# Moving eight modulation rows behind the expert loop, and ten weight slots into the second mixer

## The chip, the cores and the metric

The program runs on one core of a Trainium2 chip. The metric is the device time of one execution, in microseconds. Before the change the median of three runs is 1236.26 us (1230.97 to 1237.36). The profiled execution took 1236.48 us; its span, from the first to the last instruction, is 1234.6 us.

## The reference, cut to what matters

```python
c_act = jax.nn.silu(c)
for l in range(DEPTH):                       # DEPTH = 2, 256 tokens, width 1024, float32
    mod = (c_act @ w_mod[l] + b_mod[l])[:, None, :]
    sh1, sc1, g1, sh2, sc2, g2 = jnp.split(mod, 6, axis=-1)
    y = hybrid_mixer(x * (1.0 + sc1) + sh1, ...)
    x = layer_norm(DN_ALPHA * x + (1.0 + g1) * y, ln_g[l, 0], ln_b[l, 0])
    h = x * (1.0 + sc2) + sh2
    y = swiglu(h, ...) if l == 0 else moe_swiglu(h, ...)   # moe: top 2 of 8 experts, each 1024 x 2816 (gate, up), 2816 x 1024 (down)
    x = layer_norm(DN_ALPHA * x + (1.0 + g2) * y, ln_g[l, 1], ln_b[l, 1])
```

Each of the twelve modulation vectors is a product of one vector with a 1024 x 1024 block of w_mod. The last one, g2 of the second layer, multiplies the output of the experts and is used nowhere else.

## The kernel before, in words

The kernel goes through mixer 0, a dense feed-forward of 11 steps, mixer 1, a short routing part and the experts. All engine programs are written out by hand in order, one block for each engine, and semaphores order them against each other. SyncE (SP) issues nearly all loads.

**The modulation rows.** A modulation vector (number m) is built from 8 "rows", each a [128, 1024] block of w_mod (512 KB). VectorE multiplies each row by a column of c_act and adds it to mod_acc[m % 2] (condition_rows, L1549 to L1566; s["row_rd"] counts the rows done). TensorE then sums over the 128 partitions with a matrix of ones (gate_sum, L1012 to L1016), and VectorE adds bias and 1 (gate_apply, L1508 to L1516). Rows 64 to 71 belong to gate 10, g1 of the second layer, which the layer norm behind mixer 1 needs. Rows 72 to 79 belong to gate 11, g2 of the second layer. SP loads rows 72 to 79 in load_mod_rows (L396 to L422) behind the last weight unit of mixer 1.

**The end of mixer 1.** The output projection has four weight units (u = 12 to 15, here called i = 0 to 3). Each is split by ScalarE and VectorE into a high and a low part (conv_unit, low_unit) and used by TensorE in 3-pass products (project_out, L1104). TensorE does i = 0 and 1 for both token tiles, then gate_sum(10), then for token tile t = 0 and 1 the units i = 2 and 3, each 24 products; gate_sum(11) stands between i = 2 and 3 of t = 1. s["proj"] counts units finished for t = 1. VectorE's order (L1768 to L1781) is: rows 69 to 71, low part of i = 2, rows 72 to 75, gate_apply(10), low part of i = 3, rows 76 to 79, layer_norm(2). layer_norm (L1576) takes the four half tiles (t, h) in turn; half h = 1 of a tile needs i = 2 and 3 (for t = 0: s["wo"]; for t = 1: s["proj"]), and behind the second tile's statistics it runs gate_apply(11).

**The experts.** All weights of 8 experts stream once through a ring of 14 slots, raw_w, of 1 MB each. One expert takes 35 slots in the order: gate and up tiles of a chunk (8 slots), down tiles of the chunk before (4, 4, 3). The chunks of 2816 columns are 1024, 1024 and 768 wide. Expert loads are issued by SP: a slot is loaded again as soon as TensorE has finished with it (slot_free, L484, on s["m_used"]). The first 8 slots are the first chunk of expert 0, loaded behind s["yT_L"] >= 8; the other 6 wait for the whole mixer (s["proj"] >= 2 * NU). TensorE runs the first chunk, then a loop over pairs of experts (three rounds), then the last pair written out behind the loop (experts 6 and 7). Gate and up products are at L1399, down products at L1413. Between experts, ScalarE and VectorE add the rows of an expert (expert_rows), ScalarE stores them to DRAM (slots) and loads the tokens of a later expert (x_rows). TensorE's first down tile of an expert waits for expert_rows (s["m_y1"]). GpSimd (POOL) issues four indirect stores of tokens at the start of the experts (L647, s["sent"]) and then waits for the last pair, where it gathers the results back.

The slots overlap buffers of mixer 1: slots 0 to 4 lie on the mixer's attention buffers, slots 5 and 6 partly on buffers of rows 69 to 71, slots 8 and 9 on the raw buffers of weight units i = 0 and 1, slots 10 to 13 on those of the later units.

Of the kernel before, what the change touches and what calls it, by code (L numbers as in the profile page):

```python
# [24 lines left out]
P = 128  # L25
D = 1024
KT = D // P
T = 256
TT = T // P
# [27 lines left out]
FREE = 8  # L57
LAST1, LAST2 = NE // 2 - 1, PASSES * NE // 2 - 1
# [29 lines left out]
ROWS_DENSE, ROWS_MIX1 = 24, 64  # L88
# [12 lines left out]
           + YC + HF + [YC0, X0 + 6, X0 + 4, X0 + 5] + HF + [X0 + i for i in range(4)] + HF)  # L101
# [10 lines left out]
def hybrid_decoder(nc, x, c, w_in, w_a2, b_a, gla_norm_g, w_out, w_mod, b_mod, ln_g, ln_b,  # L112
# [3 lines left out]
    with ctx:  # L116
# [173 lines left out]
        last_S = place("last_S", [P, GROUPS, T], at=hTH_at)  # L290
        y_last = place("y_last", [P, GROUPS, 512], at=hfull_at)
# [38 lines left out]
        def rows_done(n):  # L330

            return n - sum(i < n for i in PE_ROWS)
# [51 lines left out]
        def _(sp):  # L384
# [8 lines left out]
            def load_mod_rows(*rows):  # L393

                for n in rows:
# [11 lines left out]
                    if n in (12, 72):  # L407
                        sp.wait_ge(s["pv_ps"], 2 * mix + 2)
# [4 lines left out]
                    if n == 74:  # L413
                        sp.wait_ge(s["yT_L"], 8)
# [9 lines left out]
            def unit_load(l, u):  # L424
# [10 lines left out]
                for src, at in unit_parts(l, u):  # L435
# [4 lines left out]
                               {5: (64, 65), 8: (66, 67), 9: (68, 69, 70, 71), 15: (72, 73)})  # L440
# [39 lines left out]
            load_mod_rows(*range(74, len(MOD_ROWS)))  # L480

            mg, mu, md = moe_w_gate[0], moe_w_up[0], moe_w_down[0]
            sp.wait_ge(s["yT_L"], 8)
# [6 lines left out]
            def load_gate_up(e, pr, n, c):  # L490

                f = slice(CHUNK_AT[c], CHUNK_AT[c] + CHUNK_W[c])
                for k in range(KT):
# [29 lines left out]
            load_gate_up(0, 0, -FIRST, 0)  # L523
            sp.wait_ge(s["proj"], 2 * NU)
# [19 lines left out]
        def _(pool):  # L544
# [104 lines left out]
            pool.wait_ge(s["x_ln"], 6)  # L649
            pool.wait_ge(s["m_end"], 1)  # L650
# [324 lines left out]
        def _(pe):  # L975
# [36 lines left out]
            def gate_sum(m, banks):  # L1012
# [135 lines left out]
            def mixer(l):  # L1148
# [90 lines left out]
                for t in range(TT):  # L1239
                    for i in (2, 3):  # L1240
# [10 lines left out]
                        elif l and t and i == 2:  # L1251
                            pe.wait_ge(s["row_rd"], rows_done(len(MOD_ROWS)))
                            gate_sum(11, (0, 3))
# [96 lines left out]
            pe.wait_ge(s["modT"], 11)  # L1350
# [97 lines left out]
            pe_expert(n_last, 0, True, False)  # L1448
            pe_expert(n_last, 1, True, True)
# [15 lines left out]
        def _(dve):  # L1465
# [84 lines left out]
            def condition_rows(rows):  # L1550

                for n in rows:
                    m, l, a, k = MOD_ROWS[n]
                    row, acc = mod_row[int(n >= ROWS_MIX1)][ROW_BUF[n]], mod_acc[m % 2][:]
                    dve.wait_ge(row_ld[ROW_BUF[n]], row_landed(n))
# [20 lines left out]
            def layer_norm(ph, terms):  # L1576
# [19 lines left out]
                if ph == 2:  # L1596
                    gate_apply(11, (0, 3), gate3_row)
# [122 lines left out]
            def mixer(l):  # L1720
# [52 lines left out]
                condition_rows(range(72, 76) if l else range(12, 14))  # L1773
                if l:
                    gate_apply(10, (1, 2), g_row)
                low_unit(l, NIN + 3)
                condition_rows(range(76, 80) if l else range(14, 16))
                if l == 0:
# [280 lines left out]
```

## Time and profile before

| | |
|---|---|
| median of 3 runs | 1236.26 us (1230.97 to 1237.36) |
| the profiled execution | 1236.48 us, span 1234.6 us |
| TensorE, share busy | 93% |
| VectorE, share busy | 44% |
| ScalarE, share busy | 23% |
| GpSimd, share busy | 5% |
| DMA traffic | 423.12 MB, mean 343 GB/s |
| chain that ended last | TensorE 69%, VectorE 5%, issue 2%, DMA 2%, ScalarE 1% |
| granted TensorE clock, mean | 0.984 of full speed |

The second mixer ends at about 504 us, the routing part at 521 us, and the experts fill the rest. "PE" is TensorE, "DVE" VectorE, "ACT" ScalarE, "POOL" GpSimd, "SPq" the queue of SyncE. A DMA share is the mean busy share of the core's 16 DMA engines; it reads slightly over 1 when all are busy.

### The profile page before, as it was taken

Reading aid. Unit: us, or ns where it says so; the run is one execution under the profiler, and the core shown is the slowest. Engines: PE = TensorE matmul, PEld = TensorE weight load, DVE = VectorE, ACT = ScalarE, POOL = GpSimd, SP = SyncE. Lnnn points to the kernel's source line nnn. Section 1 sums busy time; section 2 is a strip of 40 time slices with the busy share of each in tenths; the row PEclk is TensorE's granted clock in tenths of the full one; section 3 lists DMA queues with packets and bytes.
Section 4 is the critical chain, followed back from the end, with each engine's and each line's share of the span. In section 5 each row is a group of like instructions: output and inputs, shape, how many; then the busy total and the mean of one; then the engine's idle time right before and its main releaser. Section 6 shows DMA issues by size and latency. Waiting matters only on the chain.

```text
span 1234.6 us, 25919 instructions
## 1 busy us (share of the span) xinstructions
PE 1149.0 (93%) x11052; PEld 656.3 (53%) x11052; DVE 540.1 (44%) x884; ACT 283.6 (23%) x486; POOL 67.3 (5%) x118
## 2 busy tenths in 40 slices
PE   1889899999999898699999999999999999999995
PEld 1789777778878798423333324334334344343342
DVE  6799867777768999740121111021111201201226
ACT  0556343333426563310010010010100100100100
POOL 3100010000112000010000000000000000000011
PEclk9999999999999999899999999999999999999998
DMA  9974778999956747999999999999999999999991
GB/s 344 311 254 137 270 259 315 350 371 397 335 180 195 264 137 248 409 385 369 411 399 410 411 397 400 412 399 414 411 385 412 413 397 411 408 399 412 411 403 64
DMA packets 156955, 423.12 MB, mean 343 GB/s; under 512 B 21053, under 2 KB 75105, under 8 KB 145569
## 3 DMA queue, kind: packets, MB, share of 16 engines
q1 hardware_dynamic: 146720, 395.16, 83.9%
q0 software_dynamic: 6080, 20.31, 4.5%
q10 hardware_dynamic: 4032, 5.90, 1.4%
q8 instruction: 91, 1.49, 0.5%
q14 instruction: 32, 0.25, 0.1%
HBM read 405.60 MB, written 15.73 MB: 341 GB/s over the span
## 4 chain that ended last, share of the span: by engine, by line
PE 69%; DVE 5%; issue 2%; DMA 2%; ACT 1%; POOL 0%; SPq 0%; DVEq 0%; ACTq 0%
PE bank L1399 37%; PE bank L1413 18%; PE bank L347 4%; PE bank L349 3%; PE bank L348 3%; DVE mod_acc L1563 1%; DMA u_raw<-in_w_in_dram 1%; DVE u_low L1574 1%; DMA raw_u<-in_ffn_w_up_dram 1%; PE bank L982 1%; PE bank L1128 0%; PE bank L1388 0%; DVE ycat L1586 0%; DVE stats L1588 0%; DVE ycat L1585 0%
## 5 line engine op out<-in xcount | busy, mean ns | idle before, releaser
L1399 PE MATMUL bank<-raw_w,xg 128*32 128x512 f32 (+1 forms) x4608 | 468.0, 560 | 9.8 <-issue 7.2
L1399 PEld LDWEIGHTS bank<-raw_w,xg 128*32 128x32 f32 x4608 | 180.5, 110 | 289.4 <-issue 251.3
L1947 DVE TENSOR_TENSOR he<-he,bank 128x256 f32<-128x256 f32 (+1 forms) x72 | 25.6, 383 | 529.4 <-ACT he L913 529.4
L1413 PE MATMUL bank<-raw_w,heT 128*32 128x512 f32 x2112 | 237.5, 592 | 0.0
L1413 PEld LDWEIGHTS bank<-raw_w,heT 128*32 128x32 f32 x2112 | 79.9, 110 | 146.9 <-issue 145.1
L913 ACT ACTIVATE he<-bank 128x256 f32<-128x256 f32 (+1 forms) x72 | 21.2, 367 | 582.7 <-PE bank L1399 582.7
L1563 DVE SCALAR_TENSOR_TENSOR mod_acc<-mod_row,c_act,mod_acc 128x1024 f32<-128x1024 f32 x63 | 80.8, 1283 | 5.1
L347 PE MATMUL bank<-u_high,hT_H 128*128 128x256 f32 x256 | 75.1, 294 | 2.0 <-DVE u_low L1574 1.1
L349 PE MATMUL bank<-u_high,hT_L 128*128 128x256 f32 x256 | 72.2, 282 | 0.0
L348 PE MATMUL bank<-u_low,hT_H 128*128 128x256 f32 x256 | 72.1, 282 | 0.0
L347 PE MATMUL bank<-gu_H,hT_H 128*128 128x512 f32 x160 | 64.8, 405 | 0.0
L686 ACT ACTIVATE u_high<-u_raw 128x2048 fp32r<-128x2048 f32 x26 | 49.7, 1912 | 60.1 <-DMA u_raw<-in_w_in_dram 45.7
L349 PE MATMUL bank<-gu_H,hT_L 128*128 128x512 f32 x160 | 63.2, 395 | 0.0
L348 PE MATMUL bank<-gu_L,hT_H 128*128 128x512 f32 x160 | 63.1, 394 | 0.0
L1574 DVE TENSOR_TENSOR u_low<-u_raw,u_high 128x2048 fp32r<-128x2048 f32 x26 | 59.2, 2285 | 1.6 <-ACT u_high L686 1.5
L1958 DVE TENSOR_TENSOR y_sum<-y_sum,bank 32x512 f32<-32x512 f32 x48 | 32.9, 686 | 47.5 <-ACT y_sum L922 46.9
L347 PE MATMUL bank<-hT_H,u_high 128*128 128x256 f32 x176 | 50.9, 289 | 1.2 <-DVE u_low L1572 1.2
L347 PEld LDWEIGHTS bank<-u_high,hT_H 128*128 128x128 f32 x256 | 48.5, 189 | 5.8 <-DVE u_low L1574 2.3
L348 PE MATMUL bank<-hT_L,u_high 128*128 128x256 f32 x176 | 49.8, 283 | 0.0
L349 PE MATMUL bank<-hT_H,u_low 128*128 128x256 f32 x176 | 49.8, 283 | 0.0
L348 PEld LDWEIGHTS bank<-u_low,hT_H 128*128 128x128 f32 x256 | 48.5, 189 | 0.7 <-issue 0.7
L349 PEld LDWEIGHTS bank<-u_high,hT_L 128*128 128x128 f32 x256 | 48.3, 189 | 0.0
(302 smaller groups left out, 1255.9 us busy)
## 6 DMA issues: line engine op xcount, KB each, us to landing
raw_w<-in_moe_w_down_dram SPq DMA_DIRECT2D x88, 1024.0 KB, 13.0
raw_w<-in_moe_w_gate_dram SPq DMA_DIRECT2D x128, 512.0 KB, 11.3
raw_w<-in_moe_w_up_dram SPq DMA_DIRECT2D x128, 512.0 KB, 13.6
mod_row<-in_w_mod_dram SPq DMA_DIRECT2D x80, 512.0 KB, 6.9
raw_w<-in_moe_w_gate_dram SPq DMA_DIRECT2D x64, 384.0 KB, 9.8
raw_w<-in_moe_w_up_dram SPq DMA_DIRECT2D x64, 384.0 KB, 12.3
u_raw<-in_w_in_dram SPq DMA_DIRECT2D x20, 1024.0 KB, 8.0
raw_d<-in_ffn_w_down_dram SPq DMA_DIRECT2D x11, 1024.0 KB, 11.0
```

Source lines behind the costliest of these rows:

```text
L347: nc.tensor.matmul(out_ap, aH, bH, start=first, stop=False)
L348: nc.tensor.matmul(out_ap, aH, bL, start=False, stop=False)
L349: return nc.tensor.matmul(out_ap, aL, bH, start=False, stop=last)
L686: A(dst[:], src[:], ACT.Copy).then_inc(s["wH"], 1)
L913: A(he[:, g, 0:w].rearrange("s (j b c) -> s j b c", b=2, c=32), bank[g][:, 0:w].rearrange("s (j c b) -> s j b c", b=2, c=32), ACT.Silu).th ...
L982: last = mm(out_ap[p], lhsT[:, p], rhs, start=start, stop=stop)
L1399: last = mm(bank[g][32 * q:32 * q + 32, 0:2 * HALF[c]].rearrange("s (m j r) -> s m j r", m=2, r=64), xg[:, i, g, k, :], cols[:, :, :, 64 * ...
L1413: last = mm(bank[3 + g][32 * q:32 * q + 32, :], heT[(par + c) % 2][:, g, 2 * a + b, :], W[:, b, h * 512:(h + 1) * 512], start=(c == 0 and ...
L1563: last = V.scalar_tensor_tensor(out=acc, in0=row[:], scalar=c_act[:, k:k + 1], in1=acc, op0=ALU.mult, op1=ALU.add)
L1574: V.tensor_tensor(L[:], src[:], H[:].bitcast(F32), ALU.subtract).then_inc(s["wL"], 1)
L1947: V.tensor_tensor(h, h, bank[g][:, w:2 * w].rearrange("s (j c b) -> s j b c", b=2, c=32), ALU.mult).then_inc(s["m_hid"], 1)
L1958: last = V.tensor_tensor(a, a, bank[3 + g][64 * h + 32:64 * h + 64, :], ALU.add)
```

## The change

Rows 72 to 79 are no longer loaded by SP nor summed in mixer 1. GpSimd loads them into other buffers once its four indirect stores are done and the token tiles are gathered, early in the experts. VectorE sums them behind its loop over pairs of experts, fills a tile of ones, and runs gate_apply(11) between experts 6 and 7; TensorE's gate_sum(11) moves to between experts 6 and 7 as well. SP loads slots 0 to 4 once s["pv_ps"] >= 4 and s["ycat"] >= 3, slots 5 to 7 once row 71 is summed and s["yT_L"] >= 8, slots 8 and 9 once projection units i = 0 and 1 are done (proj 2 * NU - 2), and slots 10 to 13, as before, once the whole mixer is done.

```diff
--- before.py
+++ after.py
@@ -55,6 +55,7 @@
 ROWS = (PASSES * NE + 1) * SLOTS
 CLEAR_AT = (*range(5, 17), 17, 17, 18, 18, 19, 19, 20, 20, 21, 21, 22, 22)
 FREE = 8
+EARLY, NEXT = 5, 2
 LAST1, LAST2 = NE // 2 - 1, PASSES * NE // 2 - 1
 UNITC = 256
 ALPHA = (2 * DEPTH) ** 0.25
@@ -85,7 +86,7 @@
 FIRST_MOD = 2
 GATES = {2: 0, 9: 1, 10: 2, 11: 3}
 MOD_ROWS = [(m + FIRST_MOD, l, a, k) for m, (l, a) in enumerate(MODS) for k in range(KT)]
-ROWS_DENSE, ROWS_MIX1 = 24, 64
+ROWS_DENSE, ROWS_MIX1, ROWS_LAST = 24, 64, 72
 PE_ROWS = range(16, 24)
 ROWS_AT_STEP = (0, 5, 5, 5, 5, 4, 4, 4, 4, 4, 0)
 MOD_AT_STEP = {3: 5, 5: 6, 6: 7, 8: 8}
@@ -98,7 +99,7 @@
 HF, YC = [HF0, HF1], [YC0, YC1]
 ROW_BUF = (YC + YC + YC + HF + [YC0, X0 + 4, X0 + 2, X0 + 3] + HF + [X0 + i for i in range(8)] + HF
            + (HF + YC) * 10
-           + YC + HF + [YC0, X0 + 6, X0 + 4, X0 + 5] + HF + [X0 + i for i in range(4)] + HF)
+           + YC + HF + [YC0, X0 + 6, X0 + 4, X0 + 5] + YC + HF + [X0 + i for i in range(4)])
 
 PT_BANK = (6, 7, 0, 1, 3, 0)
 TOKEN_BANK = {1: ((1, 2), (4, 5)), 2: ((0, 1), (2, 3)), 3: ((1, 2), (0, 3))}
@@ -288,6 +289,7 @@
         gate3_half = place("gate3_half", [P, 512], at=hfull_at + 6144)
         back = [[place(f"back{t}_{j}", [P, D], at=over + (32 + 8 * t + 4 * j) * 1024) for j in range(2)] for t in range(TT)]
         last_S = place("last_S", [P, GROUPS, T], at=hTH_at)
+        ones_last = place("ones_last", [P, P], at=hfull_at)
         y_last = place("y_last", [P, GROUPS, 512], at=hfull_at)
 
         score, dsel, prob, relu = [score0, score1], [dsel0, dsel1], [prob0, prob1], [relu_a, relu_b]
@@ -404,14 +406,12 @@
                         sp.wait_ge(s["mod_ps"], 1)
                     if n in (6, 66):
                         sp.wait_ge(s["proj"], mix * NU + U_KEYS + 1)
-                    if n in (12, 72):
+                    if n == 12:
                         sp.wait_ge(s["pv_ps"], 2 * mix + 2)
                     if n in (9, 69):
                         sp.wait_ge(s["at_ps"], 3 * mix + 3)
                     if n == 14:
                         sp.wait_ge(s["pv_ps"], 2)
-                    if n == 74:
-                        sp.wait_ge(s["yT_L"], 8)
                     if n == ROWS_DENSE:
                         sp.wait_ge(s["hT_L"], 4)
                         sp.wait_ge(s["f_gu"], 2)
@@ -437,7 +437,7 @@
                         .then_inc(w_ld[u % 4], 16)
 
             rows_after_unit = ({3: (0, 1), 4: (2, 3), 5: (4, 5), 8: (6, 7), 9: (8, 9, 10, 11), 15: (12, 13)},
-                               {5: (64, 65), 8: (66, 67), 9: (68, 69, 70, 71), 15: (72, 73)})
+                               {5: (64, 65), 8: (66, 67), 9: (68, 69, 70, 71)})
 
             def mixer_loads(l):
                 for u in range(NU):
@@ -477,20 +477,19 @@
             mixer_loads(1)
 
 
-            load_mod_rows(*range(74, len(MOD_ROWS)))
-
             mg, mu, md = moe_w_gate[0], moe_w_up[0], moe_w_down[0]
-            sp.wait_ge(s["yT_L"], 8)
 
             def slot_free(pr, n):
 
                 if not isinstance(pr, int) or pr or n >= NRAW - FIRST:
                     sp.wait_ge(s["m_used"], pr * PER_PAIR + FIRST + n - NRAW + 1 + FREE)
 
-            def load_gate_up(e, pr, n, c):
+            def load_gate_up(e, pr, n, c, tiles=range(KT)):
 
                 f = slice(CHUNK_AT[c], CHUNK_AT[c] + CHUNK_W[c])
-                for k in range(KT):
+                for k in tiles:
+                    if n + k == NEXT:
+                        sp.wait_ge(s["proj"], 2 * NU)
                     i = (FIRST + n + k) % NRAW
                     slot_free(pr, n + k)
                     sp.dma_start(raw_w[i][:, 0, 0:CHUNK_W[c]], mg[e, :, f].rearrange("(p b) f -> b p f", b=KT)[k]).then_inc(m_ld[i], 16)
@@ -520,8 +519,13 @@
                 expert_loads(pair * 2, pr, 0, pair * 2 + 1)
                 expert_loads(pair * 2 + 1, pr, 1, following)
 
-            load_gate_up(0, 0, -FIRST, 0)
-            sp.wait_ge(s["proj"], 2 * NU)
+            sp.wait_ge(s["pv_ps"], 4)
+            sp.wait_ge(s["ycat"], 3)
+            load_gate_up(0, 0, -FIRST, 0, range(EARLY))
+            sp.wait_ge(s["yT_L"], 8)
+            sp.wait_ge(s["row_rd"], rows_done(ROWS_LAST))
+            load_gate_up(0, 0, -FIRST, 0, range(EARLY, KT))
+            sp.wait_ge(s["proj"], 2 * NU - 2)
             last = NE // 2 - 1
             with sp.Fori(0, last) as pair:
                 pair_loads(pair, pair, pair * 2 + 2)
@@ -647,6 +651,11 @@
                     pool.indirect_dma_start(slots[:, :], bass.IndirectOffsetOnAxis(ap=row_to[:, j, t:t + 1], axis=0), xb[t][:], None)\
                         .then_inc(s["sent"], 16)
             pool.wait_ge(s["x_ln"], 6)
+            pool.wait_ge(s["sent"], 16 * 2 * TT)
+            pool.wait_ge(s["xg_ps"], GROUPS)
+            for r in range(ROWS_LAST, len(MOD_ROWS)):
+                m, l, a, k = MOD_ROWS[r]
+                pool.dma_start(mod_row[1][ROW_BUF[r]][:], w_mod[l, k * P:(k + 1) * P, a * D:(a + 1) * D]).then_inc(s["brow_ld"], 16)
             pool.wait_ge(s["m_end"], 1)
             pool.wait_ge(s["row_back"], 1)
             pool.wait_ge(s["y_all"], 1)
@@ -1009,7 +1018,7 @@
                 else:
                     pe.wait_ge(s["hfull_a"], (ph - 1) * KT + 4 * t + kt - 3)
 
-            def gate_sum(m, banks):
+            def gate_sum(m, banks, ones=ones):
 
                 for h, b in enumerate(banks):
                     last = mm(bank[b][:], ones[:, 0:P], mod_acc[m % 2][:, h * 512:(h + 1) * 512], start=True, stop=True)
@@ -1248,9 +1257,6 @@
                         elif l == 0 and i == 2:
                             pe.wait_ge(s["cact"], 4)
                             sum_chunk(mod_acc[0], bank[3][:, 0:KT]).then_inc(s["mod_ps"], 1)
-                        elif l and t and i == 2:
-                            pe.wait_ge(s["row_rd"], rows_done(len(MOD_ROWS)))
-                            gate_sum(11, (0, 3))
 
             def gate_up(b, sH, sL, buf):
 
@@ -1347,7 +1353,6 @@
 
 
             transposed_tile(3, 0)
-            pe.wait_ge(s["modT"], 11)
             transposed_tile(3, 1)
 
             def tokens_back(i):
@@ -1446,6 +1451,8 @@
                 pe_expert(pr, 0, False, False)
                 pe_expert(pr, 1, False, False)
             pe_expert(n_last, 0, True, False)
+            pe.wait_ge(s["row_rd"], rows_done(len(MOD_ROWS)) + 1)
+            gate_sum(11, (6, 7), ones_last)
             pe_expert(n_last, 1, True, True)
             n_done = n_last * 2 + 2
             pe.wait_ge(s["m_S"], 1)
@@ -1552,7 +1559,10 @@
                 for n in rows:
                     m, l, a, k = MOD_ROWS[n]
                     row, acc = mod_row[int(n >= ROWS_MIX1)][ROW_BUF[n]], mod_acc[m % 2][:]
-                    dve.wait_ge(row_ld[ROW_BUF[n]], row_landed(n))
+                    if n < ROWS_LAST:
+                        dve.wait_ge(row_ld[ROW_BUF[n]], row_landed(n))
+                    else:
+                        dve.wait_ge(s["brow_ld"], 16 * (len(GATES) + KT))
                     if n:
                         dve.wait_ge(s["row_rd"], rows_done(n))
                     if k == 0:
@@ -1593,8 +1603,6 @@
                         conditioning(0, 4, bank[3][:, 0:KT]).then_inc(s["modT"], 1)
                         dve.wait_ge(s["modT"], 4)
                         norm_and_modulation(0)
-                if ph == 2:
-                    gate_apply(11, (0, 3), gate3_row)
                 for t in range(TT):
                     modulate(ph + 1, t)
                 if ph < 2:
@@ -1770,12 +1778,13 @@
                         low_unit(l, NIN + 1)
                 condition_rows(range(69, 72) if l else range(9, 12))
                 low_unit(l, NIN + 2)
-                condition_rows(range(72, 76) if l else range(12, 14))
                 if l:
                     gate_apply(10, (1, 2), g_row)
+                else:
+                    condition_rows(range(12, 14))
                 low_unit(l, NIN + 3)
-                condition_rows(range(76, 80) if l else range(14, 16))
                 if l == 0:
+                    condition_rows(range(14, 16))
                     gate_apply(2, (1, 2), g_row)
                     dve.wait_ge(s["mod_ps"], 3)
                     conditioning(0, 3, bank[0][:, 0:KT]).then_inc(s["modT"], 1)
@@ -1995,8 +2004,12 @@
                 dve_expert(pr, 0, False)
                 dve_expert(pr, 1, False)
             n_done = n_last * 2 + 2
+            condition_rows(range(ROWS_LAST, len(MOD_ROWS)))
+            dve.wait_ge(s["row_rd"], rows_done(len(MOD_ROWS)))
+            V.memset(ones_last[:], 1.0).then_inc(s["row_rd"], 1)
             V.memset(tick[:, 6:7], 0.0).then_inc(s["m_end"], 1)
             dve_expert(n_last, 0, False)
+            gate_apply(11, (6, 7), gate3_row)
             dve_expert(n_last, 1, True)
             for t in range(TT):
                 last = V.tensor_scalar(last_G[:, t].rearrange("p g (q s) -> p g q s", q=4),
```

## Rows read from the trace of the kernel before

**Rows 1.** Waits view, whole span: who waits for whom: us in total, times, longest.

```profile
PE bank L1399 <- issue: 7.2, 4, 2.6
POOL back L655 <- ACT tick L953: 643.2, 1, 643.2
```

**Rows 2.** Chain of waits in the experts, in order of time: start us, us, what.

```profile
806.45 20.60 PE bank L1399 x192
...
891.45 2.28 issue
```

**Rows 3.** Timeline of VectorE, end of mixer 1: start, us, line, operation, idle before.

```profile
481.98 4.06 DVE L1563 SCALAR_TENSOR_TENSOR mod_acc<-mod_row,c_act,mod_acc 128x1024 f32<-128x1024 f32 x3
485.96 1.28 DVE L1515 SCALAR_TENSOR_TENSOR g_row<-bank,g_row 128x512 f32<-128x512 f32 x2
...
489.36 5.46 DVE L1563 SCALAR_TENSOR_TENSOR mod_acc<-mod_row,c_act,mod_acc 128x1024 f32<-128x1024 f32 x4
...
495.20 0.69 DVE L1585 TENSOR_TENSOR ycat<-bank,g_row 128x512 f32<-128x512 f32 x1
...
503.72 0.21 DVE L1590 BATCH_NORM_AGGREGATE mv<-stats 128x2 f32<-128x12 f32 x1
```

**Rows 4.** Timeline of TensorE, end of mixer 1 to the first expert.

```profile
483.62 1.88 PE L1015 MATMUL bank<-mod_acc,ones 128*128 128x512 f32 x4
...
489.49 0.39 PE L347 MATMUL bank<-u_high,hT_H 128*128 128x256 f32 x1 [1.14 <-DVE u_low L1574]
...
495.29 1.88 PE L1015 MATMUL bank<-mod_acc,ones 128*128 128x512 f32 x4
...
499.74 0.28 PE L349 MATMUL bank<-u_high,hT_L 128*128 128x256 f32 x1
...
521.37 20.81 PE L1399 MATMUL bank<-raw_w,xg 128*32 128x512 f32 x192 [0.57 <-DVE xg L1898]
```

**Rows 5.** Timeline of the SP queue, row loads and late down tiles.

```profile
466.86 16.76 SPq L421 DMA_DIRECT2D mod_row<-in_w_mod_dram  x8
...
1173.54 1.66 SPq L506 DMA_DIRECT2D raw_w<-in_moe_w_down_dram  x2
```

**Rows 6.** Slot loads, issue to landing, issued at 512 to 514.5, 545 to 560, 1174.2 to 1175.5.

```profile
DMA to landing us min/median/max: 13.3/14.1/15.0
...
DMA to landing us min/median/max: 4.0/6.4/8.1
...
DMA to landing us min/median/max: 22.9/23.5/24.2
```

**Rows 7.** Windows: us, then PE, PEld, DVE, ACT, POOL busy, PEclk, DMA share, GB/s.

```profile
566.00:570.00 4.00, 4.00 (x44) 1.25 (x40) 2.09 (x6) 0.94 (x3) 0.00 (x0) 1.00 0.72 228
...
916.00:918.00 2.00, 2.00 (x24) 0.77 (x20) 0.42 (x2) 0.84 (x3) 0.00 (x0) 1.00 0.77 301
...
930.00:1030.00 100.00, 100.00 (x1024) 42.06 (x1020) 13.33 (x35) 6.96 (x18) 0.00 (x0) 1.00 1.02 407
```

**Rows 8.** DMA issues of the whole run: xcount, KB each, median us to landing.

```profile
raw_w<-in_moe_w_down_dram SPq DMA_DIRECT2D x88, 1024.0 KB, 13.0
raw_w<-in_moe_w_gate_dram SPq DMA_DIRECT2D x128, 512.0 KB, 11.3
...
mod_row<-in_w_mod_dram SPq DMA_DIRECT2D x80, 512.0 KB, 6.9
raw_w<-in_moe_w_gate_dram SPq DMA_DIRECT2D x64, 384.0 KB, 9.8
...
slots<-y_sum ACTq DMA_DIRECT2D x8, 384.0 KB, 6.8
```

**Rows 9.** Chain of waits, last expert, in order of time.

```profile
1197.52 10.62 PE bank L1413 x94
```

**Rows 10.** Timeline of VectorE around the start of expert 6.

```profile
1067.81 4.18 DVE L1958 TENSOR_TENSOR y_sum<-y_sum,bank 32x512 f32<-32x512 f32 x6 [6.44 <-ACT y_sum L922]
1087.59 0.75 DVE L1947 TENSOR_TENSOR he<-he,bank 128x256 f32<-128x256 f32 x2 [15.60 <-ACT he L913]
```

## The prediction

> **What bounds the kernel now.** I read the waits view first. TensorE's waits between 500 us and the end name no DMA: inside the experts they come to 7.2 us of "issue" in four pieces and little else, and POOL's one long wait runs through the experts [rows 1]. The chain in order of time is then TensorE without a break, from the first gate and up tiles at 521.37 us [rows 4] to the last down tile at 1216.9 us. One expert takes 891.45 - 806.45 = 85.0 us, and "issue" of 2.28 us stands where the loop goes back [rows 2]. So what the routing part starts earlier comes off the end one for one, as long as the weights arrive.
>
> The windows view says how far that holds. The DMA share is 1.02 in the whole of the experts, at 407 GB/s [rows 7]. One expert needs 11 down loads of 1024 KB, 32 of 512 KB and 16 of 384 KB (gate and up alike), plus 384 KB of y_sum stored and about as much of tokens read [rows 8]: 34,560 KB = 35.4 MB in 85.0 us, 416 GB/s. TensorE asks for 2% more than arrives, and the loads' time from issue to landing grows: 4.0 to 8.1 us for those issued at 545 to 560 us, 22.9 to 24.2 us at 1174 us [rows 6]. How close that is to a stop: the last expert's second chunk has four down loads, issued in the order a = 1, 0, 2, 3 and used from a = 0 on. That one is issued second, at 1173.54 us [rows 5], and lands 22.9 us later [rows 6], at 1196.4; TensorE takes it at 1197.52 [rows 9]. **The slack is 1.1 us.** The kernel is bound by TensorE, and by DMA within 1.1 us.
>
> **The end of mixer 1.** In the chain from 475 to 504 us VectorE stands alone, and eight of its row sums go. They are not worth the same.
> - Rows 72 to 75 keep VectorE until 481.98 + 4.06 = 486.0 us, and gate_apply(10) follows at once [rows 3]: 4.8 us of work. But gate_apply(10) needs gate_sum(10), which TensorE starts at 483.62 and ends at 485.5 [rows 4], in its own order behind units i = 0 and 1. Nothing in the change moves that. Worth 485.96 - 485.55 = 0.4 us; VectorE idles over 4 us instead.
> - Rows 76 to 79 take 489.36 to 494.8 us and stand straight ahead of the layer norm, which starts its first half tile at 495.20 and ends its second statistics at 503.72 + 0.21 = 503.9 [rows 3]. The low part of i = 3 ends 0.4 us earlier, at 489.0, and the norm starts today's gap of 0.45 us behind it, at 489.5. A half tile costs 2.1 us. If nothing else stood in the way it would end 5.7 us earlier.
> - What is late next is TensorE. i = 3 of t = 0 starts at 489.49, as VectorE's low part lets it [rows 4], then 0.4 us earlier, at 489.1. Up to gate_sum(11) at 495.29 [rows 4] two groups of 24 products run, 2.9 us each. So the second half tile must wait until 492.15, and its aggregate is there at 494.4. The third needs i = 2 of t = 1, done at 495.05, and ends at 497.1. The fourth needs i = 3 of t = 1: today its last product ends at 499.74 + 0.28 = 500.0 [rows 4]. It comes 0.4 us earlier, and gate_sum(11) leaves from ahead of it, which takes 1.3 us (0.33 us for each of four records; the row's 1.88 us overlap the product behind): 498.3. The half tile and the aggregate bring 500.6 instead of 503.9.
>
> **Sum of this part: -3.3 us**, not the 10 us that eight sums weigh. gate_apply(11) (1.3 us) ran while POOL, ScalarE and TensorE worked on the second tile: 0. Routing is unchanged, and the first expert starts at 518.1 us.
>
> **What the experts get.** gate_sum(11) comes between experts 6 and 7, in TensorE's unbroken chain: +1.3 us (bounds: 0.8, if it overlaps its neighbours better, and 1.9, its own busy time [rows 4]). The eight sums on VectorE: 0.75 + 7 x 1.36 = 10.3 us [rows 3]. VectorE is free there from 1067.81 - 6.44 = 1061.4 us, so expert_rows of expert 6 starts near 1072 instead of 1067.8 and ends near 1076; TensorE's first down tile waits for it only near 1087 (ScalarE and VectorE turn to the gate and up results at 1087.59) [rows 10]. 11 us are left over, cover of cost 0; without it the 10.3 us would be on the path. gate_apply(11) and ScalarE's wait for it delay the same work of expert 7 by 2.7 us, in the same gap: 0. The ones tile and the semaphore waits: 0, bound 0.2. SP's extra wait in each round is long met: 0. POOL's eight issues stand ahead of nothing until its gathers in the last pair [rows 1]: 0.
>
> **What DMA gets.** SP's stretch of 16.8 us for the eight row loads [rows 5] is replaced by slots 0 to 4, from about 468.7 us (the third ycat signal). Behind SP's four waits only weight slots queue. Slots 5 to 7 follow at 479, 8 and 9 near 483.6, 10 to 13 at 498.3; all 14 have landed by about 511, and DMA idles until the first slot is free at 521. Today TensorE has never waited for a slot, so the early loads buy no time of themselves. What they do is to take over the idle DMA time that the eight rows used, while the rows, 8 x 512 KB = 4.19 MB [rows 8], go into a stretch without any. At 407 GB/s [rows 7] they cost 10.3 us of DMA. Credits: today's last prefetches, issued at 512 to 514, land 13.3 to 15.0 us later [rows 6], 2 to 4 us after the first slot comes free, and after the change nothing is pending then (take 3.5, bounds 1 and 4); and today DMA is idle for (1.02 - 0.72) x 4 = 1.2 us at 566 and (1.02 - 0.77) x 2 = 0.5 us at 916 [rows 7], which the backlog fills. Left: 10.3 - 3.5 - 1.7 = 5.1 us, bounds 4.6 and 10.3 (no credit). Behind 916 nothing pays it off, and it meets a slack of 1.1 us in the last expert. TensorE then waits 4.0 us by 1197 us; gate_sum's 1.3 us is inside that wait, not on top.
>
> The Trainium skill, DMA: Bandwidth & Descriptors, section on the anatomy of one DMA, fits a transfer as about 2.0 us plus its bytes at 436 GB/s. By that rate the 416 GB/s asked for would be met, the backlog would drain, and the sum would be that of the first rival, to whose chance the rule gives 0.05 of its 0.25. The trace disagrees: 407 GB/s at full share and landing times that grow fourfold.
>
> The same page's arbitration paragraph says that each DMA engine takes turns between queues, a packet at a time. By it POOL's rows would halve SP's rate for some 20 us near 540, and not only queue behind it. That changes when the 10.3 us are felt, and with the 8 us at most that loads take there today [rows 6] the ring's lead of 13 slots, some 28 us or more by its tiles' times, covers it; no run yet shows it.
>
> **Forecast: 1236.5 - 3.3 + 4.0 = 1237.2, or 1237 us.** The profiled execution (1236.48) is the median of the runs within 0.3 us, so nothing is added. Own range: 1235 to 1240.
>
> **Rivals.**
> - *TensorE stays the bound.* The backlog is paid off in more places than the two I counted, or 407 GB/s isn't the limit. Then -3.3 + 1.3: 1234.5 us. For it: no DMA wait of TensorE in the experts. Against: 1.1 us of slack.
> - *The whole debt is felt (slower).* Rows on POOL's queue get no credit, and the last expert's down tiles come late: -3.3 + 10.3 - 1.1 = +5.9, 1242.4 us, and 1243.7 if gate_sum(11) falls outside TensorE's wait. It decides the sign once more than 3.3 + 1.1 = 4.4 us of debt reach 1197 us. For it: steady full share behind 580 us. Against: the idle windows are there to be filled.
> - *The chain's words are right.* VectorE's 10 us all come off, since TensorE's products move up too, and DMA follows: 1236.5 - 10.1 + 1.3 = 1227.7 us. For it: the chain names VectorE alone. Against: the starts of gate_sum(10) and of the products.
> - *The change doesn't do what it says*: SP reaches the slots no earlier, because a wait behind slots 0 to 4 holds it. Then DMA is 5 us further behind, and it is the second rival.
>
> **Chances.** Forecast 0.48, TensorE the bound 0.25, whole debt 0.17 (the last one in it), VectorE's 10 us 0.10. A measurement of this kernel tells about 0.5% (6.2 us) from no change: the three runs alone span 6.4 us. The first two cases lie inside; of the whole debt 0.10 lies beyond +6.2; VectorE's case lies beyond -6.2, and 0.03 of the forecast goes to each side for what I don't see. Faster 0.13, same 0.74, slower 0.13. Range 1230 to 1243, from the run-to-run spread below 1235 up to the whole debt.
>
> **What would show it.** The layer norm's first half tile near 489.5 us, its second aggregate near 500.8, the first gate and up tile near 518.1: right for the first part; 511 would be the fourth case. VectorE idle from 481.2 to 485.5. Landing times near 13 us instead of 4 to 8 for slots issued at 545 to 560, and over 28 us at the end; TensorE's waits naming DMA or "issue" in expert 7, some 4 us together. If TensorE's chunks stay at 20.60, 15.2 and 10.2 us to the end, the debt was paid off, and the first rival holds. The forecast is wrong if the time is outside 1230 to 1243, and its reason is wrong if TensorE never waits.

## The result, and the profile after

The changed kernel takes 1241.14 us (median of 8 runs, 1239.37 to 1246.08), the kernel before 1234.57 us beside it (8 runs, 1230.97 to 1237.36): ratio 1.0056, 95% interval 1.0043 to 1.0069. It is slower by 6.6 us (5.3 to 8.5 us by the interval), just beyond the 6.2 us that the prediction took as the bound of no change. The profiled execution took 1240.97 us, with a span of 1239.0 us (1234.6 before) and a mean granted clock of 0.987 (0.984).

TensorE's waits between 500 us and the end, changed kernel (us in total, times, longest). Before, no row named a DMA and "issue" stood at 7.2 us [rows 1]:

```profile
PE bank L1418 <- DMA raw_w<-in_moe_w_down_dram: 10.6, 7, 2.9
PE bank L1404 <- issue: 3.5, 1, 3.5
```

VectorE at the end of mixer 1, changed kernel (start us, us, line, operation, idle before), against [rows 3]. Its idle time until gate_sum(10) is there, and the layer norm moves up:

```profile
484.85 1.29 DVE L1522 SCALAR_TENSOR_TENSOR g_row<-bank,g_row 128x512 f32<-128x512 f32 x2 [4.74 <-PE bank L1024]
...
488.72 0.69 DVE L1595 TENSOR_TENSOR ycat<-bank,g_row 128x512 f32<-128x512 f32 x1
...
499.40 0.21 DVE L1600 BATCH_NORM_AGGREGATE mv<-stats 128x2 f32<-128x12 f32 x1
```

TensorE, changed kernel, first gate and up tile and the first down tile of the last expert's second chunk, against [rows 4] and [rows 9]:

```profile
515.13 5.36 PE L1404 MATMUL bank<-raw_w,xg 128*32 128x512 f32 x48 [0.57 <-DVE xg L1907]
...
1200.03 11.80 PE L1418 MATMUL bank<-raw_w,heT 128*32 128x512 f32 x96 [2.92 <-DMA raw_w<-in_moe_w_down_dram]
```

The experts start 6.2 us earlier (515.13 for 521.37) and yet reach that down tile 2.5 us later (1200.03 for 1197.52). **Between the two the changed kernel takes 684.9 us, the one before 676.2** (675.0 until the tile is there, [rows 5, 6]). All of the loss but some 1 us lies there.

Windows of the changed kernel (columns as in [rows 7]): before, the last slot loads, which stood behind the rows on SP's queue, kept the DMA engines busy past 520 us. Now the 14 slots are full near 511 us, and the engines idle until TensorE frees the first slot; behind it they are full.

```profile
508.00:512.00 4.00, 0.81 (x46) 0.59 (x49) 2.87 (x20) 3.55 (x5) 0.00 (x0) 1.00 0.58 230
512.00:516.00 4.00, 3.43 (x56) 1.59 (x52) 2.56 (x12) 0.00 (x0) 0.00 (x0) 1.00 0.02 4
516.00:520.00 4.00, 4.00 (x44) 1.30 (x40) 3.39 (x22) 0.00 (x0) 0.51 (x1) 1.00 0.23 53
524.00:600.00 76.00, 73.96 (x740) 24.60 (x736) 12.61 (x29) 6.17 (x15) 4.94 (x9) 1.00 1.02 406
600.00:1180.00 580.00, 568.81 (x5541) 210.66 (x5534) 89.26 (x198) 42.54 (x103) 5.00 (x6) 1.00 1.02 404
```

The same windows of the kernel before:

```profile
512.00:516.00 4.00, 1.15 (x46) 0.81 (x44) 2.84 (x20) 3.95 (x6) 0.00 (x0) 1.00 1.02 405
516.00:520.00 4.00, 3.69 (x44) 1.94 (x48) 1.85 (x9) 0.18 (x1) 0.00 (x0) 0.63 1.04 413
524.00:600.00 76.00, 73.96 (x724) 24.34 (x720) 18.39 (x45) 6.17 (x15) 4.25 (x4) 0.98 1.00 383
600.00:1180.00 580.00, 572.81 (x5603) 217.46 (x5599) 78.13 (x187) 42.55 (x103) 5.00 (x6) 1.00 1.02 406
```

The slot loads issued at 540 to 560 us now need 13.9 to 19.3 us to land, against 4.0 to 10.4 us before in the same stretch:

```profile
DMA to landing us min/median/max: 13.9/17.0/19.3
```

### The profile page after: what moved, and what is told of

It reads as the page before. It is cut to its first block, busy times and chain, and to the rows that moved or that the text cites. A ratio compares the mean times of both kernels' runs of the same rounds, so it can differ in the third digit from the quotient of the medians.

```text
span 1239.0 us, 25919 instructions
## 1 busy us (share of the span) xinstructions
PE 1147.1 (93%) x11052; PEld 645.5 (52%) x11052; DVE 541.1 (44%) x885; ACT 283.4 (23%) x486; POOL 70.5 (6%) x126
## 4 chain that ended last, share of the span: by engine, by line
PE 53%; SPq 12%; DMA 8%; DVE 3%; issue 2%; ACT 1%; POOL 0%; DVEq 0%; ACTq 0%
PE bank L1404 24%; PE bank L1418 14%; DMA raw_w<-in_moe_w_down_dram 6%; SPq L495 5%; SPq L496 4%; PE bank L349 4%; PE bank L351 4%; PE bank L350 4%; SPq L505 2%; DMA u_raw<-in_w_in_dram 1%; DMA raw_u<-in_ffn_w_up_dram 1%; PE bank L991 1%; DVE u_low L1584 1%; PE bank L1137 0%; PE bank L1024 0%
## 5 line engine op out<-in xcount | busy, mean ns | idle before, releaser
L1404 PE MATMUL bank<-raw_w,xg 128*32 128x512 f32 (+1 forms) x4608 | 463.2, 558 | 6.1 <-issue 3.5
L1404 PEld LDWEIGHTS bank<-raw_w,xg 128*32 128x32 f32 x4608 | 174.8, 110 | 289.6 <-issue 270.6
L1956 DVE TENSOR_TENSOR he<-he,bank 128x256 f32<-128x256 f32 (+1 forms) x72 | 25.6, 384 | 527.5 <-ACT he L922 527.5
L1418 PE MATMUL bank<-raw_w,heT 128*32 128x512 f32 x2112 | 235.1, 595 | 10.6 <-DMA raw_w<-in_moe_w_down_dram 10.6
L1418 PEld LDWEIGHTS bank<-raw_w,heT 128*32 128x32 f32 x2112 | 75.4, 110 | 163.1 <-issue 151.7
```

Of the source, the lines that this page charges most:

```text
L1404: last = mm(bank[g][32 * q:32 * q + 32, 0:2 * HALF[c]].rearrange("s (m j r) -> s m j r", m=2, r=64), xg[:, i, g, k, :], cols[:, :, :, 64 * ...
L1418: last = mm(bank[3 + g][32 * q:32 * q + 32, :], heT[(par + c) % 2][:, g, 2 * a + b, :], W[:, b, h * 512:(h + 1) * 512], start=(c == 0 and ...
L1956: V.tensor_tensor(h, h, bank[g][:, w:2 * w].rearrange("s (j c b) -> s j b c", b=2, c=32), ALU.mult).then_inc(s["m_hid"], 1)
```

## The experiments

Each was timed in five rounds beside the kernel before (medians 1234.3 to 1235.0 us). Beside the time I give one reading of each profile, the **expert interval**: from TensorE's first gate and up tile to its first down tile of the last expert's second chunk. It leaves out what the routing part does from run to run. It is one execution's, while the time is a median.

**One row in place of eight.**

```diff
 (the changed kernel)
-            for r in range(ROWS_LAST, len(MOD_ROWS)):
+            for r in range(ROWS_LAST, ROWS_LAST + 1):
...
-                    row, acc = mod_row[int(n >= ROWS_MIX1)][ROW_BUF[n]], mod_acc[m % 2][:]
+                    row, acc = mod_row[int(n >= ROWS_MIX1)][ROW_BUF[min(n, ROWS_LAST)]], mod_acc[m % 2][:]
...
-                        dve.wait_ge(s["brow_ld"], 16 * (len(GATES) + KT))
+                        dve.wait_ge(s["brow_ld"], 16 * (len(GATES) + 1))
```

> The changed kernel, but GpSimd loads only row 72 and VectorE sums that one tile eight times: seven of the eight row loads (3.67 MB, 9.0 us of DMA at 407 GB/s) are left out, all else stays, so gate 11 is a wrong sum. Theory A (the eight loads are DMA debt: every byte loaded in the experts pushes the end once TensorE waits for down tiles): TensorE's seven waits for down tiles, 10.6 us in the changed kernel's profile, go or fall under 2 us; what stays is the first expert's start 6.2 us earlier and gate_sum(11)'s 1.9 us, so about 1230 us, 3 to 5 us below before. Theory B (the time is lost in the moved sums on VectorE, gate_sum(11) or the waits they bring, not in bytes): 1239 to 1242 us as the changed kernel.

Measured: 1233.88 us, ratio 0.9989 (0.9974 to 1.0004). VectorE's eight sums, gate_sum(11) and the early slots are all in it; only 3.67 MB are not loaded, and 7.3 us are gone. Its expert interval is 1188.08 - 513.52 = 674.6 us, with one DMA wait of 2.6 us left in it. The bytes cost the time, as theory A had it, but the median is 4 us above the 1230 us that it gave; the profiled execution, 1226.90 us, is the fastest of its twelve.

**The eight rows loaded twice.**

```diff
 (the changed kernel)
-            for r in range(ROWS_LAST, len(MOD_ROWS)):
+            for r in (*range(ROWS_LAST, len(MOD_ROWS)), *range(ROWS_LAST, len(MOD_ROWS))):
...
-                        dve.wait_ge(s["brow_ld"], 16 * (len(GATES) + KT))
+                        dve.wait_ge(s["brow_ld"], 16 * (len(GATES) + 2 * KT))
```

> The changed kernel with the eight rows loaded twice into the same tiles, the second eight behind the first (result unchanged, 4.19 MB more DMA). Theory A: another 4.19 MB / 407 GB/s = 10.3 us on the end, about 1251 us, and TensorE's waits for down tiles near 21 us. If the ring hides part of it, less than 10. Theory B: 1241 us, as the changed kernel.

Measured: 1253.41 us, 1.0154 (1.0131 to 1.0177), 12.3 us above the changed kernel. Expert interval 1212.92 - 517.78 = 695.1 us: another 10.2 us for another 4.19 MB, as theory A had it. TensorE's waits named DMA for 12.9 us and VectorE's heT for another 5.1 us, 18.0 in place of 21; that the 5.1 us are waits for loads as well, as in the run with gate_sum(11) alone behind the loop (below), is likely but not shown. TensorE of that kernel in its last expert:

```profile
1201.89 9.64 PE L1408 MATMUL bank<-raw_w,xg 128*32 128x384 f32 x96 [1.97 <-DMA raw_w<-in_moe_w_up_dram]
1212.92 10.51 PE L1422 MATMUL bank<-raw_w,heT 128*32 128x512 f32 x96 [1.39 <-DMA raw_w<-in_moe_w_down_dram]
```

**The early slots undone.** Slots 0 to 7 wait again for the attention output, and 8 to 13 for the whole mixer; the rows stay in the experts. Against the changed kernel this moves slots 0 to 4 (468 to 480 us) and 8 and 9 (483 to 499 us) back.

```diff
 (the changed kernel)
-                    if n + k == NEXT:
-                        sp.wait_ge(s["proj"], 2 * NU)
...
-            sp.wait_ge(s["pv_ps"], 4)
-            sp.wait_ge(s["ycat"], 3)
-            load_gate_up(0, 0, -FIRST, 0, range(EARLY))
             sp.wait_ge(s["yT_L"], 8)
...
-            load_gate_up(0, 0, -FIRST, 0, range(EARLY, KT))
-            sp.wait_ge(s["proj"], 2 * NU - 2)
+            load_gate_up(0, 0, -FIRST, 0)
+            sp.wait_ge(s["proj"], 2 * NU)
```

> The changed kernel with the early slots undone: the first 8 slots wait for yT_L and row 71 (about 478 us), the other 6 for the whole mixer (about 497 us); the rows stay in the experts. Theory A: all 14 slots have landed by about 513 us, still ahead of the first free slot at 518, so the early loads are worth nothing here: 1240 to 1243 us, the changed kernel's time. Rival C (the early slots give DMA 10 us of lead, and the debt would be twice as large without): 1246 to 1251 us.

Measured: 1243.13 us, 1.0059 (1.0036 to 1.0083); interval 685.1 us. The early start of these seven slots is worth nothing that can be told.

**The rows loaded 345 us later**, from 882 us on (537 us in the changed kernel).

```diff
 (the changed kernel)
             pool.wait_ge(s["xg_ps"], GROUPS)
+            pool.wait_ge(s["m_used"], FREE + FIRST + 4 * PER_EXPERT)
```

> The changed kernel with GpSimd's eight row loads put off until TensorE has used 148 slots (expert 4, about 850 us). Theory A with a debt that only sums up: there is no idle DMA time to fill either way, so 1240 to 1243 us, with TensorE's waits only behind 850 us. Rival D (the two queues share the DMA engines in turn, so that a burst halves the weights' rate for 20 us, and where the backlog is larger already, TensorE stops longer): 2 us or more slower than the changed kernel. If the stretch from 540 to 800 us has idle DMA time that the rows use, this is slower too, by up to 2 us.

GpSimd's issues in this kernel:

```profile
882.42 4.29 POOL L659 DMA_DIRECT2D mod_row<-in_w_mod_dram  x8 [356.27 <-PE bank L1419]
```

Measured: 1243.57 us, 1.0067 (1.0043 to 1.0092); interval 1203.32 - 516.62 = 686.7 us. Slots issued at 540 to 560 us land in 4.2 to 7.7 us again, and one issued at 885.56 us takes 31.0. So it isn't the meeting of two queues at 540 us that costs, but the bytes, wherever in the experts they come. The median is 2.4 us above the changed kernel's and 0.4 above that of the early slots undone, timed beside it; with an interval of 3 us to each side an extra cost of rival D's 2 us is neither shown nor excluded.

**Eight more loads in the kernel before**, by GpSimd in the experts, into the same buffers as in the changed kernel and read by nobody; besides, only three waits for these loads are added near the end of the experts, long after they land.

```diff
 (the kernel before)
             pool.wait_ge(s["x_ln"], 6)
+            pool.wait_ge(s["sent"], 16 * 2 * TT)
+            pool.wait_ge(s["xg_ps"], GROUPS)
+            for b, r in zip((2, 3, 0, 1, 4, 5, 6, 7), range(72, len(MOD_ROWS))):
+                m, l, a, k = MOD_ROWS[r]
+                pool.dma_start(mod_row[1][b][:], w_mod[l, k * P:(k + 1) * P, a * D:(a + 1) * D]).then_inc(s["brow_ld"], 16)
```

> The kernel before, with GpSimd loading the eight rows a second time in the experts, where the changed kernel loads them, into tiles that nothing reads (result unchanged). Nothing else moves: TensorE's first expert stays at 521 us. This measures the debt alone, from the start of the experts that the prediction used. Theory A1 (the prediction's credits hold: the rows fill 1.7 us of idle DMA time, and 1.1 us of slack is left): 10.3 - 1.7 - 1.1 = 7.5 us slower than before, 1242 us. Theory A2 (no idle time is filled, all is felt but the slack): +9 us, 1244 us. Theory B (bytes are hidden): 1235 us.

Measured: 1246.94 us, 1.0096 (1.0069 to 1.0122), some 12 us for 4.19 MB, 3 us more than theory A2 gave. Interval 1205.99 - 520.89 = 685.1 us, 10.1 us more; where the median's other 2 us come from is open.

**The rows in the idle window.** Rows 72 and 73 stay in mixer 1. GpSimd loads 74 to 79 once the mixer's products are done, into buffers free by then; VectorE sums them behind its last norm (526 to 535 us), while TensorE runs the first chunk of expert 0 (517 to 537 us), and gate_sum(11) goes behind that chunk.

```diff
 (the changed kernel)
+            for r in range(ROWS_LAST, len(MOD_ROWS)):
+                m, l, a, k = MOD_ROWS[r]
+                if r == ROWS_LAST:
+                    pool.wait_ge(s["proj"], 2 * NU)
+                if r == ROWS_LAST + 4:
+                    pool.wait_ge(s["xb_ps"], 4)
...
             pool.wait_ge(s["zeroed"], 16 * PASSES * NE)
...
             norm_out(2)
+            condition_rows(range(ROWS_LAST, len(MOD_ROWS)))
```

> The changed kernel, with rows 72 and 73 loaded and summed in mixer 1 as before (VectorE idles there anyway), rows 74 to 79 loaded by GpSimd in the idle DMA time between the last prefetch and the first free slot (into the low half of h, which the mixer has done with, a weight buffer, and hfull), summed by VectorE behind norm_out(2) while TensorE runs the first chunk, and gate_sum(11) put where TensorE idles 2.0 us between its first two chunks. Result unchanged. Theory A: no debt in the experts and no gate_sum in the chain, so the first expert still starts near 515 us and its lead is kept as far as DMA lets it: 1229 to 1232 us, faster than before by 0.2 to 0.4%, and at or below the one-row run (1233.9). Rival E (DMA's total from 468 us on is the bound even so, since the experts start earlier but the weights don't): 1234 us, the time before.

Measured: 1233.42 us, 0.9985 (0.9968 to 1.0001), above the 1229 to 1232 us of theory A and near rival E's 1234. TensorE waits for no DMA in the experts, so rival E's reason isn't seen; its waits there are 7.9 us of "issue".

**The same with the slots late**, the waits of slots 0 to 9 as in the run with the early slots undone:

> The window kernel without the early slots (first 8 slots behind yT_L and row 71, the other 6 behind the whole mixer). Now the window's DMA time is all used, so early slots should count: without them the prefetches and the six rows end about 5 us later, past the first free slot. Theory A: 2 to 5 us slower than the window kernel. Rival: the same time, as it was with the rows in the experts.

Measured: 1233.8 us, 0.9992 (0.9976 to 1.0009), 0.4 us above the window kernel, where 2 to 5 were expected. One DMA wait of 1.0 us is back, and the interval is 1193.02 - 514.43 = 678.6 us against the window kernel's 677.0.

**The same with one of the six loads**; the missing five rows are not read from memory.

> The window kernel with only row 74 loaded and summed six times (five of the six loads left out, gate 11 is a wrong sum). If rows loaded in the idle DMA window cost nothing (theory A), the time is the window kernel's, 1233.4 us within 1 us. If even there they leave a debt, 2 us or more less.

Measured: 1232.57 us, 0.998 (0.9967 to 0.9993), within 0.9 us of the one with six. In the window the five rows, 2.6 MB, are free or nearly so; in the experts the same bytes would be 6.4 us at 407 GB/s [rows 7]. TensorE waits for no DMA in either kernel, so a debt of a us or so could hide here; the last experiment, with six rows in the window and an interval that ends with a load, shows none.

**gate_sum(11) behind the loop, in the kernel before.** Rows and slots stay as before; only the sum over partitions and gate_apply(11) move to between experts 6 and 7.

```diff
 (the kernel before)
-                        elif l and t and i == 2:
-                            pe.wait_ge(s["row_rd"], rows_done(len(MOD_ROWS)))
-                            gate_sum(11, (0, 3))
...
             pe_expert(n_last, 0, True, False)
+            pe.wait_ge(s["row_rd"], rows_done(len(MOD_ROWS)) + 1)
+            gate_sum(11, (6, 7), ones_last)
             pe_expert(n_last, 1, True, True)
```

> The kernel before, with gate_sum(11), its gate_apply and the ones tile moved behind the loop over pairs as in the changed kernel; the rows are loaded and summed in mixer 1 as before (result unchanged). The profiles so far show: where gate_sum(11) stands ahead of the loop (before, window, window without early slots, before with extra loads), TensorE stops for 2.3 to 3.9 us with no releaser at both loop-backs, with a slow stretch behind each; where it stands behind the loop (changed, one row, double rows, rows later, slots as before) it doesn't, and stops once, 3.2 to 3.5 us, at the loop's exit. Theory F (the four products less ahead of the loop shift where the loop's code lies or is fetched): both loop-back stops go, 9.3 us with their slow stretches; the exit stop, 5.4 us, and gate_sum, 1.9 us, come; net -2 us, 1232 to 1234 us, and the slack of 1.1 us takes part of it. Theory G (the stops go with the DMA backlog or the moved rows, not with the code): stops at the loop-backs as before, 1236 us.

Measured: 1236.53 us, 1.0005 (0.9989 to 1.0021): the time of before, where theory F gave 1232 to 1234. The stops did what F said all the same. TensorE's chain in order of time, first the kernel before, then this one:

```profile
716.13 2.59 issue
718.72 5.17 PE bank L1399 x31
...
891.45 2.28 issue
893.73 3.63 PE bank L1399 x31
897.36 1.93 issue
899.29 17.76 PE bank L1399 x161
...
1066.45 20.60 PE bank L1399 x192
```

```profile
716.83 20.73 PE bank L1396 x192
...
886.98 20.64 PE bank L1396 x192
...
1057.26 3.52 issue
1060.78 21.89 PE bank L1396 x188
```

The stops at both places where TensorE's loop goes back are gone, and one has come where the loop ends. The two chunks behind the loop-backs took 25.9 and 25.6 us in place of 20.6, 10.3 us of loss in all; now it is some 5 us at the exit. This kernel comes to its last gate and up tiles, the ones ahead of that down tile, 2.5 us sooner after its start than the one before (658.4 for 660.9 us), with gate_sum(11) inside. And it gains nothing, for it then stands still:

```profile
1198.22 10.51 PE L1410 MATMUL bank<-raw_w,heT 128*32 128x512 f32 x96 [2.28 <-DVE heT L1940]
```

The row names VectorE, but the part of heT that VectorE had just made belongs to the chunk behind: in the kernel before the same products started at 1197.52 [rows 9], and that work of VectorE ran from 1198.3 to 1200.0. SP issued the slot at 1177.22, the second of two loads, and it is the one that landed in 20.9 us:

```profile
1177.22 1.94 SPq L507 DMA_DIRECT2D raw_w<-in_moe_w_down_dram  x1
...
DMA to landing us min/median/max: 20.9/21.6/22.4
```

1177.2 + 20.9 = 1198.1: the load ended the wait. The interval is 676.1 us, DMA's figure again (675.0 before).

**The idle window and gate_sum(11) behind the loop together**, the lowest median of all:

> The window kernel (rows 74 to 79 loaded in the idle DMA time), with gate_sum(11) behind the loop, between experts 6 and 7, as in the changed kernel (result unchanged). Theory F: the two loop-back stops of the window kernel's profile (3.9 us each, with 4.6 us of slow stretches) go, the exit stop (5.4 us) and gate_sum (1.9 us) come: 5 us less than the window kernel if DMA keeps up, 1228 to 1231 us. Theory G: 1.9 us more than the window kernel, 1235 us. If DMA is the bound there too, 1232 to 1234 us with TensorE waiting for down tiles.

Measured: 1232.32 us, 0.9984 (0.997 to 0.9998), 2.5 us under the kernel before, as expected for the case that DMA is the bound there too; from the window kernel's 1233.42 it can't be told apart. Its interval is 1191.92 - 517.40 = 674.5 us and ends with a wait for the down load:

```profile
PE bank L1407 <- issue: 3.3, 1, 3.3
...
PE bank L1421 <- DMA raw_w<-in_moe_w_down_dram: 2.3, 1, 2.3
```

Side by side, the kernels whose interval ends with a load:

| expert interval, us | rows' MB in the experts | kernel |
|---|---|---|
| 675.0 | 0 | before (until the landing) |
| 676.1 | 0 | before, gate_sum behind |
| 674.5 | 0 | window, gate_sum behind |
| 674.6 | 0.52 | one row |
| 678.6 | about 1 | window, slots late |
| 684.9 | 4.19 | after |
| 685.1 | 4.19 | slots as before |
| 685.1 | 4.19 | before, eight more loads |
| 686.7 | 4.19 | rows later |
| 695.1 | 8.39 | rows twice |

In the kernel with the slots late, the last slots land in the experts as well as a part of the rows: SP's queue moves 262.7 MB within the interval, 260.9 before.

## Why the prediction was right and wrong

The forecast was 1237.2 us, 0.7 above the profiled execution of before; it came out 6.6 us slower in the medians, inside the range of 1230 to 1243 but outside the own range of 1235 to 1240, on the side of the second rival (1242.4 us). No change was the likeliest verdict; it is slower by just over that bound. What bounds the kernel was right. The step that failed is the credit of 5.2 us.

- **The end of mixer 1: right.** VectorE idles 4.74 us in front of gate_apply(10), as TensorE's order said, and the last aggregate stands at 499.40 for 503.72: -4.3 us, of which 0.8 was there at the start of the stretch. Net -3.5, forecast -3.3. The chain's word, 10 us of VectorE, was wrong as argued.
- **Start of the experts: 518.1 forecast, 515.13 in this execution.** Routing was 1.9 us shorter, and 1.7 of it is the clock: TensorE's gathers took 2.80 us at a granted 1.00, and 4.53 us at 0.62 in the kernel before. That is luck, and it differs between executions: of the kernels with the same code up to there, two with fast gathers (after, one row) start at 515.1 and 513.5 us, two with slow ones (rows twice, rows later) at 517.8 and 516.6.
- **gate_sum(11) and the sums: right.** 1.91 us (forecast 1.3, bounds 0.8 to 1.9) between experts 6 and 7, in a stretch whose end DMA sets; VectorE's sums were covered.
- **The credits: the step that failed.** I took 10.3 us of DMA for the rows less 5.2 of credits, and measured against the tile's landing it is 684.9 - 675.0 = 9.9 us: nearly the whole debt. The first credit, 3.5 us because no prefetch is pending when the experts start, counted only one side. From the start of the interval to its end SP's queue moves 1.8 MB less than before (259.0 for 260.9 MB), 4.5 us, and GpSimd's 4.4 MB more, 10.9 us (each at the interval's 403.5 GB/s; rows below). But in its first 5 us all queues move 0.2 MB, and 1.8 MB before: with the ring full no load can be issued until TensorE frees a slot, so DMA idles 4 us that it did not idle before. The second credit was real: the idle time near 566 us is filled, and by 60 us into the experts both kernels have moved nearly the same (22.6 and 22.3 MB), so 3.2 us of the 3.9 are made good there. Behind that, 80 to 670 us, the changed kernel moves 0.8 MB less (238.7 for 239.5), 2.0 us. Sum: 10.9 - 4.5 + 3.9 - 3.2 + 2.0 = 9.1, against the 8.7 us between these two windows (684.9 - 676.2). Why the rate is 0.4% lower at the same full share is not settled. The table says it without that sum: about 10 us for each 4.19 MB, whenever in the experts they came.

DMA queues within the expert interval (packets, MB, share of 16 engines), the kernel before and then the changed one; q1 carries SP's loads, q0 GpSimd's:

```profile
DMA packets 69460, 272.85 MB, mean 404 GB/s; under 512 B 7831, under 2 KB 10519, under 8 KB 58483
q1 hardware_dynamic: 63973, 260.85, 96.9%
...
q0 software_dynamic: 1382, 5.04, 1.9%
```

```profile
DMA packets 70192, 275.41 MB, mean 402 GB/s; under 512 B 7911, under 2 KB 10599, under 8 KB 59239
q1 hardware_dynamic: 63497, 259.04, 95.1%
q0 software_dynamic: 2592, 9.44, 3.5%
```

- **The waits: more, and sooner.** On TensorE the 8.7 us between the two intervals read as 10.6 us of waits for down tiles, less 3.7 of "issue", plus 1.9 of gate_sum(11). The forecast had some 4 us of waits, all in expert 7; they are seven, and the first (0.50 us) comes at 814.69 us. One of its signs was wrong: over 28 us from issue to landing at the end, where the loads issued at 1173 to 1184 us took 18.0 to 22.3.
- **The slack of 1.1 us: right, and it was the point.** 9.9 us of late loads less 1.1 are 8.8. Less 6.2 of earlier start, and with 1.2 more because the granted clock was 0.56 of full for 2.9 us behind the last wait (11.80 us for 10.62 [rows 9]), it is the +3.7 us at the end of the last down tile (1220.5 for 1216.9); the two profiled executions are 4.5 us apart. With starts in the middle of those seen (515.7 and 521.5) the same sum gives 4.2 of the medians' 6.6 us, whose interval is 1.6 us to each side; the other 2.4 us have no place.
- **The rule on arbitration** (the Trainium skill, DMA: Bandwidth & Descriptors, the arbitration paragraph) changed nothing that can be told, as forecast: the later rows cost the same within 2.4 us. The rate of 436 GB/s in the same page's fit was not reached: 401 to 406 GB/s over the whole interval in each kernel, whatever was added.
- **What no sum had:** that "issue" of 7.2 us in [rows 1] was a cost of TensorE that the change takes away (3.5 in the changed kernel), and that this is worth nothing while DMA ends the interval.

Shown by experiment: the price of the bytes, that seven of the ten early slots are worth nothing, the free window, the move of the stops with gate_sum(11). Argued from rows only: the split of the credits. Not tried: loading the down tile that TensorE needs first ahead of its neighbour; all seven of its DMA waits are for the first down tile of a chunk, and in the one followed to its issue that tile is loaded second, 5.3 us behind its neighbour (1180.4 for 1175.1 us).

## What to carry to other kernels

When the DMA share is full and the time from issue to landing grows along a phase, as here, expect every byte moved into the phase to be paid nearly in full, even where no engine yet waits for a load: work out the slack of the last tile, and put loads where the DMA windows read idle. A prefetch ring that is full before its first use was worth no more here for being full earlier, and a stop taken away from an engine gained nothing while the loads set the phase's length.

## What the runs showed of the hardware

TensorE stopped at its loop's branches, waiting for nothing that the profile shows, and where it stopped depended on where gate_sum(11), four products and a wait, stands. With gate_sum(11) ahead of the loop there were stops of 2.1 to 4.0 us at both loop-backs (the kernel before, the one with eight more loads, the window kernels with six loads and with one, and with late slots), none at the exit; with it behind the loop none at the loop-backs and one of 3.2 to 3.5 us at the exit (after, one row, rows twice, rows later, early slots undone, and both kernels that moved gate_sum(11) alone). Behind the stop at 716 us in the kernel before, the granted clock fell, and the products lost about as much again; behind the one at 891 it did not, and a second stop of 1.93 us followed. The window behind the first:

```profile
718.80:720.80 2.00, 2.00 (x12) 0.53 (x16) 1.96 (x4) 1.09 (x2) 0.00 (x0) 0.50 1.00 414
```

0.50 of full is the 1.2 GHz level, behind 2.59 us without work. The Trainium skill, Runtime: NRT & Kernel Launch, section on instruction fetch mechanics, says that an engine's program is fetched in blocks of fixed size, one ahead of the other, and that a taken branch out of the blocks at hand must wait for the target's block. The places of the stops agree with it, and that they move when code ahead of the loop shrinks agrees with blocks. No run here shows the cause: the trace has a queue of kind "instruction" (q8), and one packet of 0.02 MB on it falls 1 us into the stop at 1058.1 us in the changed kernel and into the one at 709.8 us in the window kernel, but such a packet comes at 717.8 us too in the kernel that moved gate_sum(11) alone, where TensorE doesn't stop.
